# Where two of the four pieces of an output weight are loaded in a fused GLA and pooling trunk: behind the third attention tile instead of ahead of it

## The reference, cut to what matters

```
h = x @ w_in;  q, k, v, g, lr = split(h)            # 512, 512, 1024, 1024, 16 columns
...                                                 # decayed keys and queries, chunks of 64 rows
o = o_intra + einsum(qe, S_prev)                    # 4 heads, 256 value columns each
o = o * rsqrt(mean(square(o)) + eps) * norm_w
y = (o * silu(g)) @ w_out                           # w_out 1024 x 1024: this weight's loads are moved
x = layernorm(alpha * x + y) * ln_g + ln_b
...                                                 # then the pooling layer, in the same manner
```

## Time and profile before

| | before |
|---|---|
| median of 3 runs | 1868.56 us (1866.0 to 1869.5) |
| the profiled execution, its own time | 1868.71 us |
| its span, first to last instruction | 1867.0 us |
| TensorE busy | 1820.8 us, 98% of the span |
| VectorE, ScalarE, GpSimd busy | 75%, 44%, 36% |
| granted TensorE clock, mean over the span | 0.994 |

### The profile page before, as it was taken

One profiled execution on the slowest core, in us unless ns is written; L12 is line 12 of the kernel. 1 busy time (PEld: TensorE's weight loads), 2 busy tenths in 40 slices (PEclk: granted clock), 3 DMA queues, 4 the chain that ended last, 5 costly groups with the idle time before them and its releaser, 6 DMA issues.

```text
span 1867.0 us, 23889 instructions
## 1 busy us (share of the span) xinstructions
PE 1820.8 (98%) x8370; PEld 1488.9 (80%) x8370; DVE 1402.9 (75%) x1677; ACT 828.3 (44%) x1278; POOL 673.9 (36%) x460
## 2 busy tenths in 40 slices
PE   9999999999999899999899999999999999999997
PEld 7778877886888788888678888878888887887885
DVE  3687756778576888887876678668899968447997
ACT  4553345556645543444454444353443444224321
POOL 0452332333131000353536555325576533223330
PEclk9999999999999999999999999999999999999998
DMA  9967683659475945765724444243465436637442
GB/s 264 280 180 238 190 279 83 148 113 261 97 154 141 305 156 165 237 226 186 265 102 153 150 134 163 68 158 124 165 200 188 169 130 221 235 135 274 177 147 101
DMA packets 282388, 334.42 MB, mean 179 GB/s; under 512 B 50465, under 2 KB 217121, under 8 KB 277665
## 3 DMA queue, kind: packets, MB, share of 16 engines
q1 hardware_dynamic: 279584, 325.60, 55.5%
q0 software_dynamic: 2688, 7.34, 1.2%
HBM read 213.34 MB, written 119.54 MB: 178 GB/s over the span
## 4 chain that ended last, share of the span: by engine, by line
PE 80%; DVE 6%; issue 3%; ACT 2%; DMA 1%; SPq 1%; POOL 1%; DVEq 0%; ACTq 0%; POOLq 0%
PE banks L248 25%; PE banks L250 24%; PE banks L249 24%; PE banks L1812 1%; PE banks L1816 1%; PE banks L951 1%; DVE m_w_lo L2833 1%; DVE m_x_lo L2847 1%; PE banks L2616 1%; PE banks L924 1%; DMA m_ahead<-x_terms 1%; DVE a_w_lo L2083 0%; PE banks L1590 0%; DMA b_raw<-x_in 0%; SPq L741 0%
## 5 line engine op out<-in xcount | busy, mean ns | idle before, releaser
L248 PE MATMUL banks<-m_x_hi,m_w_hi 128*128 128x512 f32 x1312 | 514.5, 392 | 10.6 <-DVE m_z L2908 4.4
L250 PE MATMUL banks<-m_x_hi,m_w_lo 128*128 128x512 f32 x1312 | 513.0, 391 | 0.0
L249 PE MATMUL banks<-m_x_lo,m_w_hi 128*128 128x512 f32 x1312 | 512.7, 391 | 0.0
L248 PEld LDWEIGHTS banks<-m_x_hi,m_w_hi 128*128 128x128 f32 x1312 | 246.7, 188 | 67.0 <-issue 8.3
L249 PEld LDWEIGHTS banks<-m_x_lo,m_w_hi 128*128 128x128 f32 x1312 | 246.6, 188 | 53.2 <-issue 0.7
L250 PEld LDWEIGHTS banks<-m_x_hi,m_w_lo 128*128 128x128 f32 x1312 | 246.7, 188 | 52.7
L248 PE MATMUL banks<-b_hi,h_w_hi 128*128 128x512 f32 x656 | 256.9, 392 | 6.0 <-issue 5.5
L249 PE MATMUL banks<-b_lo,h_w_hi 128*128 128x512 f32 x656 | 256.0, 390 | 0.0
L250 PE MATMUL banks<-b_hi,h_w_lo 128*128 128x512 f32 x656 | 256.0, 390 | 0.0
L2640 ACT ACTIVATE m_w_hi<-m_s 128x512 fp32r<-128x512 f32 x182 | 114.4, 629 | 204.4 <-PE banks L250 176.2
L2833 DVE TENSOR_TENSOR m_w_lo<-m_s,m_w_hi 128x512 fp32r<-128x512 f32 x182 | 161.5, 892 | 32.8 <-ACT m_w_hi L2640 31.8
(11 more groups left out here) (264 smaller groups left out, 3371.2 us busy)
## 6 DMA issues: line engine op xcount, KB each, us to landing
in_raw<-in_gla_w_in SPq DMA_DIRECT2D x128, 128.0 KB, 3.8
b_raw<-x_in SPq DMA_DIRECT2D x14, 1024.0 KB, 12.1
m_x_raw<-x_terms SPq DMA_DIRECT2D x9, 1024.0 KB, 8.8
p_in<-in_pool_w_in SPq DMA_DIRECT2D x32, 256.0 KB, 5.0
w_fused<-p_out SPq DMA_DIRECT2D x32, 256.0 KB, 4.4
x_rows<-in_x SPq DMA_DIRECT2D x64, 128.0 KB, 4.3
x_in<-in_raw SPq DMA_DIRECT2D x16, 512.0 KB, 3.8
x_in<-h_terms SPq DMA_DIRECT2D x8, 1024.0 KB, 4.2
```

Of the source, the lines that this page charges most:

```text
L248: nc.tensor.matmul(out, a_hi, b_hi, start=first, stop=False, skip_group_check=True)
L249: nc.tensor.matmul(out, a_hi, b_lo, start=False, stop=False, skip_group_check=True)
L250: return nc.tensor.matmul(out, a_lo, b_hi, start=False, stop=last, skip_group_check=True)
```

## The change

The loads of pieces 2 and 3 are taken out of `first_loads` and put into SP's step 0: piece 2 right behind the four loads of tile 2, piece 3 behind the six stores of `store_last_unit`, ahead of LayerNorm's vectors. No other instruction of any engine is changed.

```
@@ first_loads
         load_g(sp, 0, 0)
         load_g(sp, 1, 1)
         load_x(sp, 0, 0)
-        for n in (2, 3):
-            p.load_out_rows(sp, n)
@@ sync, step
                 p.load_qkv(sp, t + 2, s)
             if static and t == 0:
+                p.load_out_rows(sp, 2)
                 store_last_unit()
+                p.load_out_rows(sp, 3)
                 p.load_norm(sp)
                 load_x(sp, 1, 1)
```

## The result

The changed kernel takes 1872.65 us (median of 18 runs, 1870.31 to 1874.43), against 1868.31 us for the kernel before (18 runs, 1864.74 to 1870.52, beside it). The ratio is 1.0022, 95% interval 1.0016 to 1.0028: slower by 4.1 us, with 3.0 to 5.2 in the interval. That lies inside the stated range. It goes the way the forecast pointed, but the forecast was +0.5 us and "no change"; the time is that of the rival in which piece 3 is really late. The ratios of this document are the recorded ones; the quotient of two medians can differ from them by up to 0.0008. Two single executions, of 2691 us (the kernel before) and 4730 us (the experiment "square first"), are in no ratio.

The account below looks back on a forecast made before the run. Before 652 us the chain on DVE and ACT bounds the kernel, then PE, with only 0.31 us to give. The terms 0 + 0 + 0.5 + 0 = +0.5 us on the median 1868.56 gave 1869.1 us, range 1866.0 to 1873.6.

Parts of the forecast that it names:

- the rival in which piece 3 is really late: SP held in the stores as long as now, piece 3 travels 8.2 to 11.6 us: 1873.6, up to 1877; chance 0.13.
- Parts 1 and 2: Loads: tile 2 lands 5 us earlier, worth 0 (bounded 0 to 2.5 us); piece 2 lands at 623.4, cost 0.
- Part 4: Transfers moved past: the six stores land about 3 us earlier, the later loads have unchanged bytes ahead; cost 0.
- Part 3: ACT's part 6 waits for piece 3, issued behind the stores, delaying the square of tile 1; late by 0.5 us.
- L: Landing time of piece 3, taken as 630.4; before 629.9 it costs 0, at 634.9 it is late by 5.0 us.
- theory F: From the experiments, not the prediction: without a piece ahead of tile 2, DMA engines lose some 2 us before piece 3.
- That rival, with 0.05: TensorE's low clock stretch in 628 to 634 begins earlier or lasts longer as PE's gap grows: 1870.0; chance 0.05.
- The first rival: Piece 3 really late, SP held in the stores as long as now: 1873.6, up to 1877; chance 0.13.

Follow-up runs that it names:

- square first: Changed kernel's loads, but ACT makes tile 1's square and sum_part(2) before part 6, DVE its step 2 sums, mask and state before parts 6 and 7; 1869.02 us, ratio 1.0002.
- piece 3 home: Changed kernel with piece 3 back ahead of the attention, behind x of tile 0; piece 2 stays behind tile 2; 1867.03 us, ratio 0.9996.
- both ahead of the stores: Changed kernel with both pieces behind tile 2 and ahead of the six stores; 1868.54 us, ratio 1.0003.
- the filler: Changed kernel with x of tile 1 (0.52 million bytes) loaded in front of the attention, where the two pieces were; 1872.76 us, ratio 1.0016.
- piece 2 home: Changed kernel with piece 2 back ahead of the attention, piece 3 still behind the six stores; run twice: 1869.85 us, ratio 1.0007, and 1868.77 us, ratio 1.0006.
- held kernel: Kernel before with ACT made to wait for LayerNorm's two vectors ahead of part 6, no transfer moved; 1874.23 us, ratio 1.0038.

## Why the prediction was right, and where its size was off

**Parts 1 and 2 held, and Part 4 in its cost.** Tile 2 came sooner (v landed at 621.6, forecast 620.5) and ACT's wait for it was gone, as said; DVE's and PE's next work didn't move, and the two kernels in which nothing else is late (piece 3 home, both ahead of the stores) are at 1.000. Piece 2 cost nothing, with less cover than said: it landed at 625.3, not 623.4, and ACT waited 0.85 us, which DVE did not feel. Part 4's cost of 0 held, but its stores did not "land about 3 us earlier".

**Part 3 had the right mechanism and a wrong L.** The rule "late by L - 629.9, through parts 6 and 7 and the square" is what the trace shows: square at 635.28, one microsecond long, DVE's square_sum at 636.32, which is L + 2.1. The term of the sum that was mis-sized is "late by 0.5 us": it measured 4.7 and 3.8 us in the two traces, because L was 634.2 and not 630.4. Behind a_o_hi that is 12.3 us against 8.1, and the 4.2 us fall into two steps.

First, the stores. At 371 GB/s the piece that was no longer ahead of them should have brought their last landing forward by 2.8 us. It came at 7.9 us behind a_o_hi, against 8.1 before. The rate of the kernel before had been carried over ("at 371 GB/s they take 13.4 us"). The traffic in the 12 us up to a_o_hi + 4, the kernel before first, then the changed one:

```profile
614.30:626.30 12.00, 8.28 (x64) 7.32 (x63) 11.42 (x17) 8.70 (x13) 0.00 (x0) 1.00 1.05 386
```

```profile
613.90:625.90 12.00, 8.78 (x69) 7.82 (x68) 11.52 (x18) 10.37 (x16) 0.00 (x0) 1.00 1.00 323
```

63 GB/s less over 12 us is 0.76 million bytes, some 2 us. The seven traces with neither a piece nor the filler in front of tile 2 have 308 to 351 GB/s; the six with at least one of them have 357 to 386. A part of this is only the mix. By the traces' records of single packets, the changed kernel's 12 us hold 2329 packets of 512 bytes and the other's 1684; each takes 27 ns in both, which is 303 GB/s over 16 engines, where the median packet of 4096 bytes takes 159 ns, 412 GB/s. From these rates I estimate the mix at a fifth to a quarter of the 63 GB/s. It is not the whole reason: with piece 2 home the window holds more small packets still (3288) and moves 357 GB/s. The larger part is a tail of slow packets of 4096 bytes: 68 of 517 took over 250 ns in the changed kernel (mean 197 ns), 16 of 786 before (164 ns), 9 of 502 with piece 2 home (164 ns). SP issues nothing from 609.75, when x of tile 0 is out, to 613.33, and the prediction had warned that the queue must never be dry. But the DMA share stayed at 1.00, so theory F's reason, engines short of work, is not seen; why those packets are slow stays open.

Second, piece 3 itself. It needed 4.4 us from the last store's landing, not the 2.8 us that 1 MB takes at 371 GB/s, since transfers issued behind it moved beside it (ln_g landed 0.1 us later). The prediction's "what lands when is set by the bytes ahead of it" does not hold here. The first gate store shows it too: issued at 616.83, 0.5 us behind piece 2, it landed 0.9 us ahead of it.

The issue time played a small part. "2 MB less of backlog should let them pass sooner, so that piece 3 is issued at 625 to 626 at the latest" has a slip: piece 2 was still ahead of the stores, so it was 1 MB less. The issue came at 626.25. The landing took 8.0 us, near the 8.2 of the fastest piece before, which I had put at the far end because "those four stood in a backlog that here has been worked off". It had not been: at 626.25 the last store was still 3.5 us from landing. The range held because its upper end had been taken from those rows; the sum alone would not have reached the result.

**The clock took part in another way than its rival said.** That rival, with 0.05, was the low stretch behind the scores beginning earlier or lasting longer. PE's gap there did grow, to 3.40 us, but the low stretch behind it lies as before, from about 6 to 13 us behind a_o_hi. A second one came behind PE's wait of 4.17 us. TensorE's stretches in the changed kernel, from 634 us on:

```profile
634.00:638.00 4.00, 0.33 (x1) 0.00 (x0) 2.28 (x4) 3.01 (x5) 0.00 (x0) 0.89 1.02 372
638.00:642.00 4.00, 3.50 (x9) 2.83 (x10) 3.47 (x8) 3.05 (x6) 0.00 (x0) 0.57 0.67 253
```

PE idles for nearly all of 634 to 638, and from 638 to 642 the granted clock is 0.57 on average, mostly the lower level of 1.2 GHz; in the kernel before, it was 1.00 from 636 to 642. By the Trainium skill, "TensorE: Matmul & The Clock Gate", Part 1, the clock follows how busy the PE has recently been, and the trace agrees. It does not agree with a simpler rule, that every such gap brings the lower clock: with both pieces ahead of the stores PE also idled for 3.41 us behind the scores and came back at 1.00. The stretch splits accordingly. Step 2's mean starts 4.35 us late (16.58 us behind a_o_hi against 12.23), and from it to step 3's mean PE takes 19.05 us instead of 17.89, of which 0.31 us had been idle. So about 1.2 of the 5.5 us are the clock's. In the held kernel the same two terms are 4.36 and 1.77 us. Piece 3 need not be late for this: both pieces ahead of the stores has 19.13 us in the second term.

**The chances.** "Within 0.2%" had 0.84 and "slower" 0.12. The result, 0.16 to 0.28%, has the border of 0.2% (3.7 us) inside its interval and lies beyond it in the middle. The first rival's price, 1873.6, was the better forecast. It was put at 0.13 by an argument, "travel time was the backlog", that no row of the kernel before bore out, while two rows spoke for it: the 8.2 to 11.6 us to landing and SP's 9.6 us in the stores.

## What to carry to other kernels

Before a load is moved behind a group of stores on the same queue, take its landing time from its siblings' rows (8.2 us at the least here, and 8.0 measured), not from bytes over a rate measured in another order: the move itself changed the rate, and transfers issued behind the load took their share. Ask what stands behind the first instruction that wants the load, on its engine and on the engines that wait for it; here moving four instructions back (parts 6 and 7 on two engines) made nearly the same late landing almost free. And of the orders tried, none was better than issuing both pieces in SP's pause ahead of tile 2.

## What the runs showed of the hardware that was not expected

The time that SP is held in stores falls less than the bytes ahead of them. Six 256 KB stores held it, singly for 0.5 to 2.9 us, for 9.3 us in the changed kernel and 9.6 before, with 1 MB less ahead. Over eleven traces it was 9.6 to 10.7 us with both pieces ahead of the stores (four traces) and 8.0 to 9.3 us with one (seven): 1.5 us less on average, where 1 MB at 371 GB/s is 2.8 us.

DMAs on one queue did not land in the order of their issue, nor one after the other: a 256 KB store issued 0.5 us behind a 1 MB load landed 0.9 us ahead of it, and a 512 KB load issued 0.8 us behind piece 3 landed 0.1 us behind it.

The rate of nearly the same transfers depended on what preceded them: 323 and 327 GB/s in the changed kernel, with nothing in front of tile 2, 357 to 382 with one piece, 361 with a 0.5 MB filler, 386 with two. The share of busy DMA time hardly changed (1.00 against 1.05), so the engines were not idle. A part is the mix of packet sizes; the rest is that more packets of 4096 bytes took over 250 ns (68 of 517 against 16 of 786). Why they do stays open.
